# Modulation columns of a two-block transformer: partial sums turned by TensorE, or row sums taken by VectorE from turned weights

## The reference, cut to what matters

```python
silu_c = jax.nn.silu(c)
silu_cc = jax.nn.silu(c_ctx)
for l in range(DEPTH):
    mod = silu_c @ w_mod[l] + b_mod[l]        # (1024) @ (1024, 6144)
    mod_c = silu_cc @ w_mod[l] + b_mod[l]
    sh1, sc1, g1, sh2, sc2, g2 = jnp.split(mod[:, None, :], 6, axis=-1)
    ...
    h = h + g1 * mix
    h = h + g2 * sq_relu_mlp(modulate(rms_norm(h, norm2_g[l]), sh2, sc2), w_ff1[l], w_ff2[l])
```

## Time and profile before

| | us |
|---|---|
| median of 3 runs (lowest, highest) | 2261.74 (2258.91, 2265.05) |
| the profiled execution | 2265.22 |
| its span, first to last instruction | 2263.3 |
| PE busy | 2171.4 (96%), granted clock 0.990 |
| DVE busy | 1641.7 (73%) |
| ACT busy | 886.0 (39%) |
| POOL busy | 719.8 (32%) |
| DMA read | 338.04 MB, 150 GB/s over the span |

### The profile page before, as it was taken

How to read it: one execution, slowest core, us unless ns; L and a number is a source line. 1 busy time by engine, 2 the same in 40 slices (tenths; PEclk the granted TensorE clock), 3 DMA queues, 4 the chain that set the end, 5 groups by cost and what they waited for, 6 DMA issues and landing times.

```text
span 2263.3 us, 31613 instructions
## 1 busy us (share of the span) xinstructions
PE 2171.4 (96%) x12654; PEld 1828.7 (81%) x12654; DVE 1641.7 (73%) x2368; ACT 886.0 (39%) x1345; POOL 719.8 (32%) x455
## 2 busy tenths in 40 slices
PE   6999999999999989999998999999999999999997
PEld 2887777788888778898987887777888888859997
DVE  6565667997768994867999876767877684685443
ACT  3323333222333332544443446753223333364453
POOL 0000210232344520213455373333333455213344
PEclk9999999999999999999999999999999999999999
DMA  9432225455555463354765542122655553614552
GB/s 317 148 100 77 66 81 180 149 169 185 189 195 192 164 191 117 103 168 150 260 220 190 168 150 84 66 75 84 209 191 174 198 183 75 144 38 140 177 187 75
DMA packets 268027, 341.17 MB, mean 151 GB/s; under 512 B 31057, under 2 KB 181465, under 8 KB 267625
## 3 DMA queue, kind: packets, MB, share of 16 engines
q1 hardware_dynamic: 266704, 334.92, 46.1%
q10 hardware_dynamic: 1176, 4.23, 0.6%
HBM read 338.04 MB, written 1.08 MB: 150 GB/s over the span
## 4 chain that ended last, share of the span: by engine, by line
PE 76%; DVE 14%; issue 4%; ACT 3%; POOL 2%; DMA 1%; SPq 0%; DVEq 0%; ACTq 0%; POOLq 0%
PE PS L745 22%; PE PS L747 21%; PE PS L746 21%; DVE bias L1811 5%; DVE w_l L1781 3%; DVE work L1911 1%; PE PS L855 1%; DVE a_l L1921 1%; PE PS L1175 1%; PE PS L992 1%; POOL a_l L2431 1%; PE PS L1001 1%; PE PS L1015 1%; PE PS L1201 1%; ACT w_h L1374 1%
## 5 line engine op out<-in xcount | busy, mean ns | idle before, releaser
L745 PE MATMUL PS<-a_h,w_h 128*128 128x512 f32 (+1 forms) x2624 | 909.3, 347 | 29.2 <-DVE w_l L1781 16.7
L746 PE MATMUL PS<-a_l,w_h 128*128 128x512 f32 (+1 forms) x2624 | 896.4, 342 | 0.0
L747 PE MATMUL PS<-a_h,w_l 128*128 128x512 f32 (+1 forms) x2624 | 896.4, 342 | 0.0
L1781 DVE TENSOR_TENSOR w_l<-ring,w_h 128x1024 fp32r<-128x1024 f32 (+1 forms) x416 | 578.9, 1432 | 166.8 <-ACT w_h L1374 166.0
L1374 ACT ACTIVATE w_h<-ring 128x1024 fp32r<-128x1024 f32 (+1 forms) x416 | 409.0, 1033 | 524.8 <-PE PS L747 520.8
L745 PEld LDWEIGHTS PS<-a_h,w_h 128*128 128x128 f32 x2624 | 500.7, 191 | 116.4 <-issue 34.3
L747 PEld LDWEIGHTS PS<-a_h,w_l 128*128 128x128 f32 x2624 | 500.9, 191 | 56.3
L746 PEld LDWEIGHTS PS<-a_l,w_h 128*128 128x128 f32 x2624 | 501.1, 191 | 53.2
L1811 DVE SCALAR_TENSOR_TENSOR bias<-ring,silu,bias 128x512 f32<-128x512 f32 x518 | 448.9, 917 | 4.1 <-DMA ring<-in_w_mod 0.5
L2431 POOL TENSOR_TENSOR a_l<-hid,a_h 128x2048 fp32r<-128x2048 f32 (+1 forms) x60 | 231.2, 3853 | 251.0 <-ACT a_h L1398 251.0
L2446 POOL TENSOR_TENSOR hid<-hid 128x256 f32<-128x256 f32 (+1 forms) x128 | 172.1, 1347 | 403.1 <-ACT hid L1356 403.1
(11 more groups left out here) (223 smaller groups left out, 2575.8 us busy)
## 6 DMA issues: line engine op xcount, KB each, us to landing
ring<-in_w_ff SPq DMA_DIRECT2D x64, 1024.0 KB, 5.6
ring<-in_ffn_w SPq DMA_DIRECT2D x64, 1024.0 KB, 5.5
ring<-in_w_mod SPq DMA_DIRECT2D x48, 1024.0 KB, 5.3
ring<-in_ada_w SPq DMA_DIRECT2D x48, 1024.0 KB, 5.3
ring<-in_w_in SPq DMA_DIRECT2D x42, 1024.0 KB, 5.3
ring<-in_mlstm_w_in SPq DMA_DIRECT2D x12, 1024.0 KB, 6.3
ring<-in_w_o SPq DMA_DIRECT2D x8, 1024.0 KB, 5.5
ring<-in_w_attn_out SPq DMA_DIRECT2D x4, 1024.0 KB, 6.0
```

The lines of the kernel that those rows point to most:

```text
L745: nc.tensor.matmul(out, stat[0], mov[0], start=start, stop=False, **kw)
L746: nc.tensor.matmul(out, stat[0], mov[1], start=False, stop=False, **kw)
L747: return nc.tensor.matmul(out, stat[1], mov[0], start=False, stop=stop, **kw)
L1781: V.tensor_tensor(w_l[:, n % 2, c], ring[:, slot_of[split_raw[n]], c], w_h[:, n % 2, c].bitcast(F32), ALU.subtract).then_inc(s_wl, 1)
```

## The change

For most blocks the raw tile now comes from a turned copy of the weights (the host stores `w_mod` and `ada_w_2` also transposed): 256 output columns as 2 x 128 partitions, each with all 1024 input values in a row. A modulation column is then one row sum: DVE multiplies a row of weights by the silu vector, which has been copied to all partitions (`cond`), and sums it in the same instruction (`tensor_tensor_reduce`, 1024 elements), straight into `mod`. PE and PSUM have no part in it, and `mod_columns` only adds the bias vector. The blocks that stay as they were are 0 to 9 of layer 0 and blocks 0 and 1 of layer 2 (`by_dots` is false).

`cond` lies in `work[:, 4:6, :]`, which other phases overwrite, so it is loaded three times (1 MB each) by SP, in the second step of the output products `w_o` of layers 0 and 1 and `m_out` of layer 2. Its source is made once: PE turns `silu` (one transpose), ACT copies it and issues four small stores.

`spread` is always false now: in layer 1's feed-forward a raw tile is taken whole in every other step. In the norm at layer 1's start PE does six more idle transposes (`stay_awake`).

```diff
-        spread = layer == 1
+        spread = False
...
+        dots = bias[:, :, :].rearrange("p v n -> p (v n)")
+        cond = work[:, 4:6, :]
+        silu_rows = work[0:32, 5, 0:P]
...
+        def by_dots(key):
+            return key[:2] > (0, 9) and key[:2] not in ((2, 0), (2, 1))
...
+                c0 = 512 * b + LAT * half
                 tiles.append((what, count,
-                               [(lambda t: view4(t), rows(w[512 * half:512 * half + 512, 512 * b:512 * b + 512]))]))
+                              [(lambda t: t.rearrange("p (j k) -> p j k", j=2), rows(wT[c0:c0 + LAT, :]))
+                               if by_dots(key) else
+                               (lambda t: view4(t), rows(w[512 * half:512 * half + 512, 512 * b:512 * b + 512]))]))
...
+            def load_cond(ph):
+
+                if ph["name"] == "m_out":
+                    sp.wait_ge(s_mpt, 4 * MH)
+                else:
+                    sp.wait_ge(s_xl, ph["x"])
+                sp.wait_ge(s_srs, 64)
+                src = io["silu_rows"][(ph["layer"] + 1) // 2].rearrange("v k p -> v (k p)")
+                sp.dma_start(cond, src.partition_broadcast(P)).then_inc(s_cond, 16)
...
+                    if ph.get("name") in ("w_o", "m_out") and st is ph["steps"][1]:
+                        load_cond(ph)
...
-                if st["modu"] is None:
+                if st["modu"] is None or by_dots(st["modkey"]):
                     return
...
                             mod_unit(late_step)
+                            stay_awake(6, 5)
...
+            def mod_dots(key, ks):
+
+                layer, b, half = key
+                nv = mod_vectors(key)
+                w = raw_slot(dve, mod_raw[key]).rearrange("p (j k) -> p j k", j=2)
+                if ks[0] == 0:
+                    dve.wait_ge(s_cond, 16 * (2 if layer == 2 and 1 < b < 10 else 3 if layer > 1 else 1))
+                    if half:
+                        dve.wait_ge(s_mtile, mod_count[key] - 1)
+                for i in range(2 * nv) if len(ks) == 4 else ks:
+                    j, v = divmod(i, nv)
+                    out = w[:, j, :]
+                    if v < nv - 1:
+                        out = dots
+                        if dotted[0]:
+                            dve.wait_ge(s_dve, dotted[0])
+                    ins = V.tensor_tensor_reduce(out, w[:, j, :], cond[:, v, :], 1.0, 0.0, ALU.mult, ALU.add,
+                                                 mod[:, layer % 2, 4 * b + 2 * half + j, v:v + 1])
...
+        out[name + "T"] = f[name].transpose(0, 2, 1)
```

More of the change, by code:

```diff
@@ L269, in build @@
         s_mcsum = sem("mod_block_summed")
+        s_srow = sem("silu_turned")
+        s_srs = sem("silu_rows_stored")
+        s_cond = sem("silu_broadcast")
         s_mcol = sem("mod_columns_ready")
@@ L452, in push_mods @@
                 w = io["w_mod" if layer < 2 else "ada_w_2"][layer % 2]
+                wT = io["w_modT" if layer < 2 else "ada_w_2T"][layer % 2]
                 mod_raw[key] = len(tiles)
@@ L614, in build @@
         mod_unit_of = {st["modkey"][:2]: st["modu"] for ph in plan for st in ph["steps"] if st["modkey"]}
+        summed = {}
+        for ph in plan:
+            for st in ph["steps"]:
+                if st["modkey"] and not by_dots(st["modkey"]):
+                    summed[st["modu"]] = len(summed) + 1
         mod_before = {}
@@ L619, in build @@
                 for key in st["mods"]:
-                    if key[2] == 0 and before is not None and key[:2] != (0, 3):
+                    if key[2] == 0 and before is not None and key[:2] != (0, 3) and not by_dots(key):
                         mod_before[key] = before
-                if st["modu"] is not None and st["modkey"] not in by_pe:
+                if st["modu"] in summed and st["modkey"] not in by_pe:
                     before = st["modu"]
@@ L811, in first_tiles, with stay_awake @@
                     mod_unit(st)
-            def stay_awake(n):
+            def stay_awake(n, spare_bank=7):
                 for _ in range(n):
-                    nc.tensor.transpose(PS[:, 7, 0:P], ident[:, :], ident[:, :])
+                    nc.tensor.transpose(PS[:, spare_bank, 0:P], ident[:, :], ident[:, :])
             def row_products(st):
@@ L932, in _ @@
                     mod_unit(b3, columns=1)
+                    nc.tensor.transpose(PS[0:32, 5, 0:P], silu[:, :, :, :].rearrange("p b k v -> p (b k v)"), ident[:, :]
+                                        ).then_inc(s_srow, 1)
                     pe.wait_ge(s_const, CONST)
@@ L1467, in _ @@
                     for i, st, u in steps_of(ph):
+                        if ph["l"] == 0 and i == 3:
+                            act.wait_ge(s_srow, 1)
+                            step(nc.scalar.activation(silu_rows, PS[0:32, 5, 0:P], ACT.Copy))
+                            for b in range(2):
+                                for v in range(2):
+                                    nc.scalar.dma_start(io["silu_rows"][b, v], silu_rows[16 * b + v:16 * b + 16:2, :]
+                                                        ).then_inc(s_srs, 16)
                         if ph["l"] == 1:
@@ L1602, in _ @@
                             nc.scalar.activation(Bc[:, :, :], Bc[:, :, :], ACT.Exp, scale=-1.0).then_inc(s_gr, 1)
-                            act.wait_ge(s_mcsum, ph["steps"][4]["modu"] + 1)
+                            act.wait_ge(s_mcol, ph["steps"][4]["modu"] + 1)
                             act.wait_ge(s_dec, 16)
@@ L1792, in mod_tile @@
             def mod_tile(key, st, last, ks=range(4)):
+                if by_dots(key):
+                    mod_dots(key, ks)
+                    return
                 layer, b, half = key
@@ L1797, in mod_tile @@
                 if half == 0 and key in mod_before and ks[0] == 0:
-                    dve.wait_ge(s_mcsum, mod_before[key] + 1)
+                    dve.wait_ge(s_mcsum, summed[mod_before[key]])
                 if half and ks[0] == 0:
@@ L1817, in mod_tile @@
                             ins.then_inc(s_dve, 1)
+            dotted = [0]
+            def mod_dots(key, ks):
[15 more added lines that the diff above has]
+                                                 mod[:, layer % 2, 4 * b + 2 * half + j, v:v + 1])
+                    if i == 2 * nv - 1:
+                        ins.then_inc(s_mtile, 1)
+                    elif v < nv - 1:
+                        steps[0] += 1
+                        dotted[0] = steps[0]
+                        ins.then_inc(s_dve, 1)
             def mod_columns(st):
@@ L1824, in mod_columns @@
                 nv, mu = mod_vectors(st["modkey"]), st["modu"]
-                dve.wait_ge(s_mcsum, mu + 1)
+                if by_dots(st["modkey"]):
+                    dve.wait_ge(s_mtile, mod_count[st["modkey"]])
+                else:
+                    dve.wait_ge(s_mcsum, summed[mu])
                 m = mod[:, layer % 2, :, :]
@@ L1830, in mod_columns @@
                     src = PS[:, 2 + b // 2, 0:8].rearrange("p (c n) -> p c n", n=2)
+                elif by_dots(st["modkey"]):
+                    src = sums
                 else:
@@ L2090, in branches @@
                                                    op0=ALU.add, op1=ALU.mult).then_inc(s_free[bank_of[uu + b]], 1)
+                    if ph["l"] == 0:
+                        dve.wait_ge(s_srs, 64)
                     rowmax(0)
@@ L2623, in lay_out @@
         out[name] = f[name]
+    for name in ("w_mod", "ada_w_2"):
+        out[name + "T"] = f[name].transpose(0, 2, 1)
     out["swa_sink_2"] = f["swa_sink_2"].reshape(-1)
@@ L2640 @@
     io["decay_rows"] = nc.dram_tensor("decay_rows", (MH, 2, ALL), F32, kind="Internal").ap()
+    io["silu_rows"] = nc.dram_tensor("silu_rows", (2, 2, KC, P), F32, kind="Internal").ap()
     io["out"] = nc.dram_tensor("outT", (D, LAT), F32, kind="ExternalOutput").ap()
```

2 lines of the change are left out of this document (1 added, 1 removed).

## The result

The changed kernel takes 2236.78 us in the median (2236.09 to 2237.88, 4 runs), the kernel before beside it 2262.64 (2258.91 to 2265.05, 4 runs): ratio 0.9892, 95% interval 0.9879 to 0.9905. That is 25.9 us less, where 30.7 was forecast (2231).

A forecast was written before the change was run, and what follows sets the result against it. PE was taken to set the pace, except in layer 1's ff2, bound by DVE. Terms -22.5 - 7 - 1 (end of layer 0's ff2) + 0.5 = -30 gave 2231 us against the median of 2261.7; range 2217 to 2246.

The forecast's parts named there:

- Term 1: Between PE's tiles: removing the transposes saves 21.1 us, and 1.4 of waits in layers 0 and 2; -22.5 us.
- The period of two steps: Sign of being right: two steps of layer 0's ff1 take 21.8 us, where they took 22.65.
- Rival 4: PE's transposes were hidden, so removing them only moves the wait; little but DVE's saving remains: 2252 us, chance 0.04.
- Term 2: Layer 1's ff2, bound by DVE: cheaper row sums and no sums from PSUM, -7 us.
- the part on whole tiles: Whole tiles in every other step: taken as 0; a miss in ff1 would cost +4 to +7 us.
- the limit of 11.3 to 12.9 us against 11.3 to 11.9: ff1 with whole tiles: DVE's path with POOL's squares against two steps of PE, judged at the limit.
- The row sum's price: DVE's row sum over 1024 elements: 1.17 us start to start, bounded by 1.13 and 1.33.
- Rival 2: DVE's row sum runs at half rate, about 2.2 us: about +96 us, 2358; chance 0.06.
- Rival 1: POOL interrupts DVE's row sums less, layer 1's ff2 falls toward the floor: up to 16 us more, 2215; chance 0.11.
- Rival 3: Layer 1 gives back: late tile in ff1, nothing of Term 2; +7 and +7, 2245 us; chance 0.09.
- `ff2` at 112 to 114 us with DVE still without idle time: Sign of being right, for layer 1's ff2.
- Term 3: Added work, with three 1 MB loads, hidden or up to 1 us late in layer 1's w_o: +0.5 us.

The follow-up runs named there:

- e3: The changed kernel with as many transposes as before put back on PE, of the identity and waited for by nothing: 2254.93 us, ratio 0.9955.
- e1: The changed kernel with layer 1's feed-forward in halves again (spread true there): 2230.18 us, ratio 0.9848 to the kernel before.
- e4: The changed kernel without the six extra idle transposes in layer 1's first norm: 2235.27 us, ratio 0.9871.
- e9: e1 with whole tiles in layer 1's ff1 alone, halves only in its ff2: 2230.78 us, ratio 0.9868.
- e2: The kernel before with whole tiles in layer 1 (spread false) and nothing else: 2263.3 us, ratio 1.0.
- e5: e1 with blocks computed in layer 1's feed-forward and m_in back on transposed copies and multiply-adds: 2241.36 us, ratio 0.9907.
- e7: e1 with block (2, 8) computed in m_in instead of layer 1's ff2: 2237.44 us, ratio 0.9892.
- e10: e1 with half block (2, 5, 1) moved from layer 1's ff2 to its ff1: 2230.35 us, ratio 0.986.

## Why the prediction was right, and where it was not

**Term 1** (PE's transposes, -22.5) was right. `e3` puts the transposes back and nothing else, and pays 18.2 us in the medians; 21.1 was the sum for them. By stages it is 18.2 where the sum had 20.2 (layer 0, layer 1's `ff1`, layer 2), nothing in `m_in` (0.9 in the sum) and 1.0 in layer 1's `ff2` (nothing in the sum). The period of two steps came out as computed. Rival 4, that they were hidden, is out.

**Term 2** (DVE's own work in layer 1's `ff2`, -7) was right as a saving and wrong as a gain. `e1`, with the order of before, shows DVE's busy time down by 7.0 and the stage by 4.0; `ff1` and `ff2` together are down by 9.0, where 9.6 was forecast. After the change DVE's busy time was down by more, `ff2` by 0.6 and both together by 4.4.

**The step that failed** is in the part on whole tiles: "In `ff2` DVE is behind in either order and never idle, so the order costs nothing." DVE is behind on average, but not in every step. A whole tile holds it for 4.6 us, or for more where POOL works (6.8 us from 1202.59), and the split that is due meanwhile comes late; PE waits for it. Then DVE has no sums left and catches up, until it must wait for ACT, which waits for PE. A wait of PE and a wait of DVE take turns, where halves spread the work so that both are short: PE's longest wait for a split is 3.3 us with whole tiles (4.1 in `e4`) and 1.4 with halves (2.3 in `e9`). The stage sums of before hid this, since DVE showed 113.3 of 114 us busy; `e2` shows that the same order made 7.7 us of such idle time there too. Layer 1's two stages in all kernels that bear on it (us):

| kernel | raw tiles | sums | `ff1` | `ff2` | both |
|---|---|---|---|---|---|
| before | halves | multiply-adds | 105.5 | 120.2 | 225.7 |
| `e5` | halves | multiply-adds | 104.0 | 120.3 | 224.3 |
| `e2` | whole | multiply-adds | 104.9 | 122.9 | 227.8 |
| changed | whole | row sums | 101.7 | 119.6 | 221.3 |
| `e4` | whole | row sums | 101.8 | 120.3 | 222.1 |
| `e9` | whole, halves | row sums | 101.8 | 114.9 | 216.7 |
| `e1` | halves | row sums | 100.5 | 116.2 | 216.7 |

The order costs 4.6 to 5.4 us with the row sums and 2.1 to 3.5 with the multiply-adds. In the sum it stood at 0; with what was measured for Term 2 and the order together in `ff2` (-0.6), the sum would have been -24 instead of -30. That 25.9 came out, nearer to the forecast, is in part luck: "all else" gave 1.8 us where 0.5 was to be lost, and its largest item is the program's start.

There is a second loss in it. PE's clock by stretches after the change, around one of those waits:

```profile
1185.00:1188.40 3.40, 3.40 (x30) 3.40 (x30) 3.40 (x5) 1.00 (x2) 2.32 (x1) 1.00 0.63 251
1188.40:1192.90 4.50, 1.19 (x9) 0.87 (x7) 4.50 (x4) 2.95 (x3) 4.42 (x4) 1.00 0.24 64
1192.90:1199.70 6.80, 6.11 (x29) 6.02 (x29) 6.76 (x6) 0.00 (x0) 6.09 (x3) 0.50 0.81 273
```

PE had been full, waited 3.3 us and soon after 0.7 more, both for a split, and was granted 1.2 GHz (0.50) over these 6.8 us: 29 matmul records in 6.1 us, 0.21 each, where they start 0.12 us apart at 2.4 GHz. Such a stretch costs up to 29 x 0.09 = 2.6 us, and the mean clock of the stage is 0.90 to 0.93 in the profiled kernels with whole tiles (`e2`, changed, `e4`) and 0.94 to 0.96 in those with halves (before, `e5`, `e1`, `e9`). How much of the 3.4 us between `e1` and the changed kernel in `ff2` is this, and how much the waits themselves, the runs don't part.

**In `ff1`** the limit of 11.3 to 12.9 us against 11.3 to 11.9 was judged rightly: whole tiles cost 1.3 us there at most, and with `e9` nothing that can be told, not 4 to 7.

**The row sum's price** was right, 1.14 us against 1.17. Rival 2 is out: both sources are fp32 in SBUF, the sum is accumulated, and 1024 elements take 0.01 us more than a split without an accumulator (1.13). The Trainium skill, "Vector Engine (DVE) Microarchitecture Reference", section 7, says that the scalar-tensor-tensor form with two SBUF sources that are not bf16 runs at half throughput. The trace does not agree for this kernel's multiply-add, which is of that form (0.66 us for 512 elements). The row sum is printed as a custom instruction; that form with an accumulator no run here has.

**Rival 1** (POOL interrupts DVE less) came true for the sums and brought nothing, since the splits took the waiting over. DVE's groups in the stage `ff2`, before:

```profile
L1811 DVE SCALAR_TENSOR_TENSOR bias<-ring,silu,bias 128x512 f32<-128x512 f32 x50 | 60.3, 1262 | 0.0
L1781 DVE TENSOR_TENSOR w_l<-ring,w_h 128x1024 fp32r<-128x1024 f32 x32 | 43.5, 1398 | 0.4 <-ACT w_h L1374 0.4
```

after the change:

```profile
L1821 DVE TENSOR_TENSOR w_l<-ring,w_h 128x1024 fp32r<-128x1024 f32 x32 | 54.7, 1753 | 7.6 <-ACT w_h L1407 7.6
L1880 DVE CUSTOM_DVE_ANT_0 ring<-ring,work 128x1024 f32<-128x1024 f32 x14 | 25.2, 1801 | 0.0
L1880 DVE CUSTOM_DVE_ANT_0 bias<-ring,work 128x1024 f32<-128x1024 f32 x14 | 23.2, 1658 | 0.1
```

and in `e1`:

```profile
L1821 DVE TENSOR_TENSOR w_l<-ring,w_h 128x1024 fp32r<-128x1024 f32 x31 | 59.6, 1960 | 0.0
```

Take off what the instructions need undisturbed (0.66, 1.13 and 1.14 us each, 0.44 for the six L1809): the sums' waiting falls from 30 us to 16, the splits' grows from 7 to 18, and to 25 in `e1`. This is an estimate from these rows, and that all of it is waiting for POOL is not shown. In all it is 38, 35 and 40 us: the prediction left the sum as it was, and rightly, but it moved onto the instruction that PE waits for. The rival's own argument put the sums' waiting at a third of DVE's time; 30 of 113 us is a quarter. POOL waits more too. A group of its squares in that stage, before:

```profile
L2414 POOL TENSOR_TENSOR work<-h 128x256 f32<-128x256 f32 x7 | 7.5, 1072 | 0.0
```

and after, 1.59 us each, the same in `e1`:

```profile
L2491 POOL TENSOR_TENSOR work<-h 128x256 f32<-128x256 f32 x7 | 11.2, 1594 | 0.0
```

**Rival 3** (layer 1 gives back) came true by a part: next to nothing of Term 2, but not the late tiles in `ff1`. Of the prediction's signs, "`ff2` at 112 to 114 us with DVE still without idle time" did not come true: the whole stage took 119.6 (120.2 before, of which its 114 are a part) with 10.6 us of idle time. **Term 3**: in layer 1's `w_o` ACT waited for PE and DVE alone, never for `ring`, so the load of `cond` is hidden; `e4` shows that the idle transposes decide nothing that the time tells.

## What to carry to other kernels

Work that rides beside a pipeline of double-buffered tiles should be priced also by the longest piece that holds the engine between two deadlines, not by its sum alone. An engine that looks 99% busy over a stage can still idle in it once its work comes in larger lumps, so look at what one step must hold before calling an order free. Moving work out of such a stage pays only if the neighbour has idle time on the same engine: `e7` took 5.6 us out and got 8.5 back. And when a stage's border is an event on one engine, check that the border itself did not move: most of what `e10` seemed to shift was that.

## What the runs showed of the hardware

A DVE instruction of 8 elements per partition can take as long as what POOL is doing. DVE's and POOL's timelines after the change, the first two rows DVE's:

```profile
1209.37 2.35 DVE L1821 TENSOR_TENSOR w_l<-ring,w_h 128x1024 fp32r<-128x1024 f32 x2
1211.64 2.33 DVE L1912 TENSOR_TENSOR mod<-mod,vec 128x8 f32<-128x8 f32 x1
...
1210.50 3.45 POOL L2508 TENSOR_TENSOR a_l<-hid,a_h 128x1024 fp32r<-128x1024 f32 x1 [3.29 <-ACT a_h L1431]
```

L1912 ends at 1213.97, POOL's instruction at 1213.95. The Trainium skill, "SBUF — State Buffer", section "SBUF: two separate sides", describes this as an exclusive lock on a shared port pair, held for the whole instruction by whoever starts first; the trace agrees here, with 2.33 us for the small add. POOL's instruction paid too: it began at 1210.50, beside DVE's second split, and took 3.45 us; the same instruction at 1204.76 began just ahead of DVE's next one and took 2.45, and then it was DVE's row sum that lasted 3.41. The row sum came out at its lower bound: the accumulator's read of 0.08 us lies wholly within the 1.14, 0.01 above the split.
